# A two-layer attention block and a mixture of experts on one core: the first three head tiles multiply the residual without its norm, and large buffers share one start modulo 512 bytes

## Chip, cores and metric

One core of a Trainium2 chip. The metric is the device time of one execution in microseconds; the number of a kernel is the median over its runs. All arithmetic that matters is FP32, with matrix products as three products of operands split in a rounded high part and a low rest.

## What is computed

The reference runs `first_block` (two layers) and `second_block` (one layer) on 512 tokens of width 1024. The change touches the two layers of the first block. Cut to what matters:

```python
def rms_norm(x, g):
    y = xf * lax.rsqrt(jnp.mean(xf * xf, axis=-1, keepdims=True) + EPS)
    return (y * g.astype(jnp.float32)).astype(x.dtype)

def token_mixers(u, w_in, ...):
    proj = u @ w_in
    qa, ka, va, qi, ki, wi, qb, kb, vb, gate_a, gate_b = jnp.split(proj, ...)
    qa = apply_rope(rms_norm(qa.reshape(...), g_qa), cos, sin)
    qi = apply_rope(qi.reshape(bsz, length, H_I, D_I), cos, sin)
    ki = apply_rope(ki, cos, sin)
    ...
for i in range(DEPTH):
    u = rms_norm(h, g_mix_norm[i])
    h = h + token_mixers(u, w_in[i], ...)
    h = h + conv_ffn(rms_norm(h, g_ffn_norm[i]), w_up[i], conv_w[i], conv_b[i], w_down[i])
    ple_gate = jax.nn.sigmoid(rms_norm(h, g_ple_norm[i]) @ w_ple_gate[i])
    h = h + ple_gate * (p[i].astype(h.dtype) @ w_ple_proj[i])
```

The norm of a token is one number, so a product of the residual with its gain but without the norm can be scaled afterwards: (h * g * n) @ w = ((h * g) @ w) * n, with n one factor for each token. The indexer's key (ki) and queries (qi) have no norm of their own; they are the first three head tiles.

## The kernel before

**Layout.** Activations stand transposed: 128 channels on the partitions, 512 tokens along the row, eight slices k for a width of 1024. hT is the residual, XH and XL are the high and low part of what is multiplied. Weights come as blocks of up to 1 MB (eight slices of 256 columns, BLK = 2048 words a partition). SyncE loads block n into raw[n % 3] (`load_to`, L2320) once the last tile of block n-3 is done; ScalarE copies it to wh, rounded (`cuts_to`, L1948); VectorE subtracts it from raw, which gives wl in place (`cuts_to`, L1368). A tile (`tile`, L895) is 128 output channels: for each k three matmuls of 128x128 by 128x512, wh by high, wh by low, wl by high, all into one PSUM bank; it is 24 matmuls at a depth of eight slices. wh or wl is the stationary operand, the activation the moving one.

**Order of the work.** Each engine has one hand-written program, in which functions of the same name meet through semaphores (`Signal`, `Banks`). Nothing is planned by costs: what an engine does next is what its program says next. TensorE's program (L1283 on) is for each layer: `norm_sums` (column sums of squares, 8 products of one column, L950), `norm_row` (spreads the 512 norm factors over the partitions, L963), `first_projections` (L1009), `attention` with the gate tiles between its steps (L1118), `branches` (L1190), `linear` (output), `ffn` (L1220), `embed` and `ple` (L1248, L1276). `keep_warm` (L890) puts filler matmuls where TensorE would be idle.

**The norm ahead of a layer.** ScalarE squares the slices (`square_of`, L1955), VectorE adds them (`add_to_norm`, L1378); after `norm_sums` VectorE scales, ScalarE takes the root, VectorE the reciprocal (`root`, L1392 and L1963). Then `rms` (VectorE L1399, ScalarE L1985) works through the eight slices: VectorE writes U = h * gain * norm (L1407), ScalarE rounds U into XH (L1969), VectorE subtracts for XL (L1415). The first projection tile takes slice k when XL of k is there (`fresh`, L901), the later ones without a wait.

**first_projections.** s counts 16 head tiles: ki, qi0, qi1, ka, then queries and keys of both attentions. Tiles 0 to 2 are copied to the arena by ScalarE as they are (L2043); from tile 3 on it squares and scales them (L2045, L2046). After tile 2 TensorE multiplies two columns for the lambdas (L1062), which VectorE made at the head of its own `first_projections` (L1468 to L1470). SyncE swaps the halves of each head by DMA (`swap_halves`, L2329), GpSimd multiplies by sin and cos (L2309, L2310), VectorE adds (`rope`, L1560). The index scores need tiles 0 to 2 from s = 5 on; VectorE then picks the top 256 keys by repeated maximum and replacement (`choose`, L1539).

**Where things lie.** Per partition in this order: hT, XH, XL (16384 bytes each), raw, wh (24576 each), cst (2692 words), sml (849 words), arena (NAR = 15120 words), slots (94 words), owner (16), scr (17 x 512 words), tiny. Each starts at a multiple of 32 bytes. The arena is reused by stage: heads, values and masks at the word offsets of L661 to L663; the two parts of the attention outputs (OBH, OBL and, over QB and KB, oah, oal); in the feed-forward and gated stages QH, QL (words 0 and 4096), the moving operands of the up-projections and of `ple`; the embedding's high part at 12288. The down-projections and all input projections take XH and XL. In the expert stage at the end nearly all of these buffers are places for expert weights (PARTS, L798).

```python
        KI, QI, OBH, OBL = 0, 512, 0, 2048
        KA, WV, QA, MB = 4096, 4608, 4880, 6928
        QB, KB, VB = 8976, 11024, 13072
```

Of the kernel before, what the change touches and what calls it, by code (L numbers as in the profile page):

```python
# [17 lines left out]
D = 1024  # L18
KT = 8
# [148 lines left out]
def program(nc, A, out, sizes, cparts, stop=None):  # L168
# [3 lines left out]
    with ExitStack() as ctx:  # L172
# [11 lines left out]

        at = here()
# [18 lines left out]
        NAR = 15120  # L204
# [4 lines left out]
        owner = sb("owner", [1, 16], I32)  # L209
        at = here()  # L210
# [354 lines left out]
        u_done = Signal(sem("u_done"), [(r, k) for r in (0, 3, 6) for k in range(8) if r >= 6 or k < 7])  # L565
        xkeys = []
        for li in layers:
            xkeys += [(r, k) for r in (3 * li, ("mix", li), 3 * li + 1, 3 * li + 2) for k in range(8)]
# [83 lines left out]
        def u_ready(r, k):  # L652
            return u_done((r, k)) if r >= 6 or k < 7 else bank.empty(("spread", r))
# [8 lines left out]
        KA, WV, QA, MB = 4096, 4608, 4880, 6928  # L662
        QB, KB, VB = 8976, 11024, 13072  # L663
# [26 lines left out]
        RROW, UP = S_(5), [S_(3), S_(4), S_(6)]  # L690
        pp, ph, pl = A3(8192, 8), R3(12288, 2), R3(13312, 2)
# [188 lines left out]
        def tensor_engine(pe):  # L880
# [14 lines left out]
            def tile(key, w, c, xs, fresh=None, warm=0, among={}):  # L895

                ps = opened(key)
                keep_warm(ps, warm)
                h, l = w
                for i, (k, hi, lo) in enumerate(xs):  # L900
# [4 lines left out]
                    mm = pe.matmul(ps[0:c.stop - c.start, :], l[:, k, c], hi, start=False, stop=i == len(xs) - 1)  # L905
                    if i in among:
                        among[i]()
# [42 lines left out]
            def norm_sums(r):  # L950
# [3 lines left out]
                keep_warm(ps, 3 if r and r % 3 == 0 else 0)  # L954
# [53 lines left out]

            def first_projections(li):  # L1009
                n0 = PER_LAYER * li  # L1010
                def two_scores(pair):
# [11 lines left out]
                for s in range(21):  # L1023
# [5 lines left out]
                    if s < 16:  # L1029
                        n = n0 + (s // 2 if s < 4 else s // 2 + 1)  # L1030
                        if s % 2 == 0:
                            split(n)
                        c = slice(128 * (s % 2), 128 * (s % 2) + 128)
                        tile(("win", li, s), weights(n, 256), c, xs, (lambda k: x((3 * li, k))) if s == 0 else None,
                             2 if s == 0 and li else 0, {1: lambda: head_rows(li, s - 1), 5: lambda: head_columns(li, s - 1)}
# [7 lines left out]
                    elif s < 20:  # L1043
# [239 lines left out]
            pe.wait_ge(c_first, 16)  # L1283
            for li in layers:
                n0 = PER_LAYER * li
                norm_sums(3 * li)
                norm_row(3 * li)
# [77 lines left out]
        def vector_engine(dve):  # L1365
# [33 lines left out]
            def rms(r, gain):  # L1399
                root(("sum", r), 4, 1.0 / D, EPS, normcols(r), nroot, r, nrec)  # L1400
                key = ("spread", r)
                dve.wait_ge(*bank.full(key))
# [382 lines left out]
            def ple(m, n0, r):  # L1785
# [3 lines left out]
                def gated(k):  # L1789
# [7 lines left out]
                    if k >= 2:  # L1797
                        add_to_norm(r, k - 1)
# [1946 lines left out]
```

## Time and profile before

| | |
|---|---|
| median of 3 runs | 2735.25 us (2733.56 to 2735.48) |
| profiled execution, its own time | 2737.47 us |
| its span | 2736.1 us |
| TensorE, VectorE, ScalarE, GpSimd busy | 2581.3, 1508.6, 1094.3, 153.8 us |
| mean granted TensorE clock | 0.98 |
| first layer | 0 to about 864 us |
| second layer | about 864 to 1707 us |
| second block up to the experts | 1707 to 2395 us |
| experts | 2395 to 2640 us |
| end | 2640 to 2736 us |

PE is TensorE's matmuls, PEld its weight loads (they overlap), DVE VectorE, ACT ScalarE, POOL GpSimd, SPq SyncE's queue. Matmuls are pipelined: the listed duration of one is longer than the step from its start to the next start. A clock of 1.00 is 2.4 GHz; it can be granted at 2.4 or at 1.2 GHz.

### The profile page before, as it was taken

To read this page: it belongs to the slowest core of one execution; us is meant where nothing else is said; L and a number is where in the kernel's file an instruction comes from. 1 tells how busy PE (TensorE), PEld (TensorE's weight loads), DVE (VectorE), ACT (ScalarE), POOL (GpSimd) and SP (SyncE) were. 2 spreads that over 40 slices of the span, in tenths; PEclk is the share of its full clock that TensorE was granted. 3 is DMA by queue.
4 is the path that set the end of the run, shared out by engine and by line. 5 is a ranking of instruction groups with operands and counts; after the bars stand their busy time and mean duration, and the time that the engine had idled before them with its cause. 6 is when DMAs were issued, how large, how long until landed. Compare 5 with 4: busy or idle time off the path is not lost.

```text
span 2736.1 us, 35790 instructions
## 1 busy us (share of the span) xinstructions
PE 2581.3 (94%) x14600; PEld 1906.8 (70%) x14600; DVE 1508.6 (55%) x2596; ACT 1094.3 (40%) x1725; POOL 153.8 (6%) x133
## 2 busy tenths in 40 slices
PE   5999999999999989999999999999999989999777
PEld 4777678888887777778888887766766658733226
DVE  4787556646566698555747475445434525412227
ACT  3436544333344425653424243354332324233235
POOL 1310000000000320000000000000000000022210
PEclk9999999999999999999999999999999989999998
DMA  4322232232221322232222222312111124699991
GB/s 153 116 81 85 89 123 100 93 100 101 89 97 62 122 99 81 97 116 100 93 100 101 93 93 93 123 45 88 47 51 43 36 97 147 250 373 394 399 373 73
DMA packets 70283, 342.97 MB, mean 125 GB/s; under 512 B 11618, under 2 KB 12514, under 8 KB 37220
## 3 DMA queue, kind: packets, MB, share of 16 engines
q1 hardware_dynamic: 64996, 332.22, 34.2%
q0 software_dynamic: 5120, 8.40, 0.9%
q8 instruction: 119, 1.95, 0.3%
q14 instruction: 48, 0.39, 0.0%
HBM read 312.26 MB, written 28.31 MB: 124 GB/s over the span
## 4 chain that ended last, share of the span: by engine, by line
PE 78%; DVE 8%; SPq 4%; ACT 4%; DMA 3%; issue 2%; POOLq 0%; DVEq 0%; ACTq 0%
PE bank L903 14%; PE bank L905 14%; PE bank L904 14%; SPq L3461 4%; PE bank L1093 4%; PE bank L1095 3%; PE bank L1094 3%; PE bank L2431 2%; PE bank L3328 2%; PE bank L1137 2%; DVE wl L1374 2%; PE bank L1167 1%; PE bank L1157 1%; DMA raw<-in_WE 1%; ACT wh L1952 1%
## 5 line engine op out<-in xcount | busy, mean ns | idle before, releaser
L1374 DVE TENSOR_TENSOR wl<-raw,wh 128x2048 fp32r<-128x2048 f32 (+1 forms) x165 | 368.3, 2234 | 168.8 <-ACT wh L1952 167.7
L903 PE MATMUL bank<-arena_rounded,wh 128*128 128x512 f32 x1056 | 418.8, 397 | 3.4 <-DVE arena_rounded L1624 3.2
L905 PE MATMUL bank<-arena_rounded,wl 128*128 128x512 f32 x1056 | 417.5, 395 | 0.0
L904 PE MATMUL bank<-arena_rounded,wh 128*128 128x512 f32 x1056 | 417.4, 395 | 0.0
L1952 ACT ACTIVATE wh<-raw 128x2048 fp32r<-128x2048 f32 (+1 forms) x165 | 303.3, 1840 | 174.2 <-DMA raw<-in_W 174.1
L903 PE MATMUL bank<-XH,wh 128*128 128x512 f32 (+1 forms) x760 | 303.0, 399 | 4.8 <-DVE XL L1415 4.7
L904 PE MATMUL bank<-XL,wh 128*128 128x512 f32 (+1 forms) x760 | 297.5, 391 | 0.0
L905 PE MATMUL bank<-XH,wl 128*128 128x512 f32 (+1 forms) x760 | 297.2, 391 | 0.0
L903 PEld LDWEIGHTS bank<-arena_rounded,wh 128*128 128x128 f32 x1056 | 199.1, 189 | 52.8 <-issue 5.2
L905 PEld LDWEIGHTS bank<-arena_rounded,wl 128*128 128x128 f32 x1056 | 199.0, 188 | 47.4
L904 PEld LDWEIGHTS bank<-arena_rounded,wh 128*128 128x128 f32 x1056 | 199.2, 189 | 46.8
L1093 PE MATMUL bank<-XH,wh 128*128 128x512 f32 (+1 forms) x408 | 186.6, 457 | 0.0
L903 PEld LDWEIGHTS bank<-XH,wh 128*128 128x128 f32 (+1 forms) x760 | 142.8, 188 | 50.3 <-issue 12.6
L905 PEld LDWEIGHTS bank<-XH,wl 128*128 128x128 f32 (+1 forms) x760 | 142.8, 188 | 31.5
L904 PEld LDWEIGHTS bank<-XL,wh 128*128 128x128 f32 (+1 forms) x760 | 143.0, 188 | 29.3 <-issue 0.2
L1095 PE MATMUL bank<-XH,wl 128*128 128x512 f32 (+1 forms) x408 | 163.1, 400 | 0.0
L1094 PE MATMUL bank<-XL,wh 128*128 128x512 f32 (+1 forms) x408 | 163.1, 400 | 0.0
L1747 DVE TENSOR_TENSOR scr<-bank,scr 128x512 f32<-128x512 f32 x88 | 60.8, 691 | 140.2 <-PE bank L905 140.1
L2071 ACT ACTIVATE scr<-scr,tiny 128x128 f32<-128x128 f32 (+3 forms) x160 | 89.3, 559 | 102.3 <-DVE tiny L1599 102.1
L2167 ACT ACTIVATE scr<-scr,sml 128x512 f32<-128x512 f32 x88 | 71.8, 816 | 140.2 <-DVE scr L1747 140.2
L1093 PEld LDWEIGHTS bank<-XH,wh 128*128 128x128 f32 (+1 forms) x408 | 78.1, 191 | 50.6 <-issue 34.3
L3413 DVE TENSOR_TENSOR scr<-bank,scr 64x512 f32<-64x512 f32 x32 | 21.9, 683 | 163.8 <-ACT scr L3390 163.8
(540 smaller groups left out, 4191.2 us busy)
## 6 DMA issues: line engine op xcount, KB each, us to landing
raw<-in_W SPq DMA_DIRECT2D x153, 1024.0 KB, 4.8
arena<-in_WE SPq DMA_DIRECT2D x31, 1024.0 KB
wh_full<-in_WE SPq DMA_DIRECT2D x15, 1024.0 KB
raw<-in_WE SPq DMA_DIRECT2D x15, 1024.0 KB
gsave<-scr SPq DMA_DIRECT2D x48, 256.0 KB
scr<-gsave SPq DMA_DIRECT2D x48, 256.0 KB, 4.0
XH_full<-in_WE SPq DMA_DIRECT2D x10, 1024.0 KB
XL_full<-in_WE SPq DMA_DIRECT2D x10, 1024.0 KB
```

What stands on the lines that cost most here:

```text
L903: pe.matmul(ps[0:c.stop - c.start, :], h[:, k, c], hi, start=i == 0, stop=False)
L904: pe.matmul(ps[0:c.stop - c.start, :], h[:, k, c], lo, start=False, stop=False)
L905: mm = pe.matmul(ps[0:c.stop - c.start, :], l[:, k, c], hi, start=False, stop=i == len(xs) - 1)
L1093: pe.matmul(o, h[:, k, c], hi, start=k == 0, stop=False)
L1094: pe.matmul(o, h[:, k, c], lo, start=False, stop=False)
L1095: mm = pe.matmul(o, l[:, k, c], hi, start=False, stop=k == KT - 1)
L1374: w_lo.inc(dve.tensor_tensor(wl[:, i % 3, 0:k], raw[:, i % 3, 0:k], wh[:, i % 3, 0:k].bitcast(F32), ALU.subtract), i)
L1747: bank.emptied(dve.tensor_tensor(u, bank.ap(key), RROW, ALU.mult), key)
L1952: w_hi.inc(act.activation(wh[:, i % 3, 0:k], raw[:, i % 3, 0:k], ACT.Copy), i)
L2071: sexp.inc(act.activation(dst[:, 0:n], dst[:, 0:n], ACT.Exp, scale=-1.0, bias=c, accum_out=c_sum), (m, s, e))
L2167: aff.inc(act.activation((FV if which else FG)[q % 2][i], UP[(4 * q + 2 * which + i) % 3], ACT.Identity, scale=K(f"cw2{li}", f), bias=K(f" ...
L3461: moe.e_in[n % RING].inc(sync.dma_start(moe.place(i, part_), expert(i, part_)), n)
```

## The change

**Starts of the buffers.** 128 bytes are put ahead of hT and ahead of the arena, 64 ahead of scr, the arena becomes 112 words longer, and its parts QA, MB, QB, KB, VB move up by 112 words.

**Tiles 0 to 2 of each layer.** A new `raw_high` (ScalarE) and `raw_low` (VectorE) split h * gain, without the norm, into XH and XL: for the first layer at the very start as x lands, for the second between the steps of the gated projection before it. TensorE's new `raw_projections` multiplies tiles 0 and 1 together, slice by slice, then tile 2. `norm_sums` and `norm_row` move in between: in the second layer the sums after slice 3 and the spread after slice 5 of the two tiles, in the first layer the sums after both tiles and the spread after slice 3 of tile 2. VectorE copies the spread row to WROW (scr slice 15), makes U from it as before, and scales tiles 0 to 2 by it as it takes them out of PSUM (`raw_head`), two between slices, the third at the end. ScalarE overwrites slice k of XH when tile 2 has used it (`raw_used`). Tile 3 is now the first that takes the normed XH and XL. The lambda products stay at the head of VectorE's `first_projections`, which comes after all of `rms`, and TensorE's lambda matmul at s = 2 is now ahead of its first tile in that loop. The filler ahead of the norm sums and of tile 0 in the second layer goes. The root's table is loaded ahead of the first norm. SyncE loads the first weight block after the first quarter of x and the second block ahead of the constants, and block n0+3 ahead of the first swaps.

```diff
+        sb("front", [128, 32])
         at = here()
         hT = sb("hT", [128, KT, T])
...
-        NAR = 15120
+        NAR = 15232
+        sb("gap", [128, 32])
...
         owner = sb("owner", [1, 16], I32)
+        sb("behind", [128, 16])
...
-        KA, WV, QA, MB = 4096, 4608, 4880, 6928
-        QB, KB, VB = 8976, 11024, 13072
+        KA, WV, QA, MB = 4096, 4608, 4992, 7040
+        QB, KB, VB = 9088, 11136, 13184
...
+            def raw_projections(li):
+                n0 = PER_LAYER * li
+                r = 3 * li
+                keys = [("win", li, i) for i in range(2)]
+                split(n0)
+                ps = [opened(key) for key in keys]
+                h, l = weights(n0, 256)
+                for k, hi, lo in xs:
+                    pe.wait_ge(*x((("raw", r), k)))
+                    for i, key in enumerate(keys):
+                        c = slice(128 * i, 128 * i + 128)
+                        pe.matmul(ps[i], h[:, k, c], hi, start=k == 0, stop=False)
+                        pe.matmul(ps[i], h[:, k, c], lo, start=False, stop=False)
+                        mm = pe.matmul(ps[i], l[:, k, c], hi, start=False, stop=k == KT - 1)
+                        if k == KT - 1:
+                            bank.filled(mm, key)
+                    if li and k == 3:
+                        norm_sums(r)
+                    if li and k == 5:
+                        norm_row(r)
+                if li == 0:
+                    pe.wait_ge(c_first, 16)
+                    norm_sums(r)
+                split(n0 + 1)
+                tile(("win", li, 2), weights(n0 + 1, 256), slice(0, 128), xs, None, {} if li else {3: lambda: norm_row(r)},
+                     lambda mm, k: raw_used.inc(mm, (r, k)))
...
-                    if s < 16:
+                    if 3 <= s < 16:
...
+            def raw_low(r, k):
+                dve.wait_ge(*xh((("raw", r), k)))
+                x.inc(dve.scalar_tensor_tensor(out=XL[:, k, :], in0=hT[:, k, :], scalar=K(f"gmix{r // 3}", k),
+                                               in1=XH[:, k, :].bitcast(F32), op0=ALU.mult, op1=ALU.subtract), (("raw", r), k))
+            def raw_head(li, s):
+                key = ("win", li, s)
                 dve.wait_ge(*bank.full(key))
+                bank.emptied(dve.tensor_tensor(head_at(s), bank.ap(key), WROW, ALU.mult), key)
+            def rms(li):
+                r = 3 * li
+                norm_row(r, WROW)
                 for k in range(KT + 1):
...
+                    if k in (4, 5):
+                        raw_head(li, k - 4)
+                raw_head(li, 2)
...
+            for k in range(8):
+                if k == 2:
+                    cuts_to(0)
+                raw_low(0, k)
+            cuts_to(1)
             for k in range(1, 7):
                 add_to_norm(0, k)
...
+            def raw_high(r, k):
+                act.wait_ge(*h_ready(r, k))
+                xh.inc(act.activation(XH[:, k, :], hT[:, k, :], ACT.Copy, scale=K(f"gmix{r // 3}", k)), (("raw", r), k))
...
                 for k in range(KT):
+                    act.wait_ge(*(raw_used((r, k)) if k < KT - 1 else bank.full(("win", li, 2))))
                     high((r, k), k, U[k % 3], u_ready(r, k))
...
             for i in range(4):
                 quarter_in[i].inc(sync.dma_start(hT[:, 2 * i:2 * i + 2, :], A["xT"][:, 2 * i:2 * i + 2, :]), "x")
-            sync.dma_start(sml[:, :], A["small"]).then_inc(s_in, 16)
+                if i == 0:
+                    sync.dma_start(sml[:, :], A["small"]).then_inc(s_in, 16)
+                    load_to(0)
+            load_to(1)
             sync.dma_start(cst[:, 0:384], A["consts"][:, 0:384]).then_inc(c_first, 16)
-            load_to(0)
             sync.dma_start(cst[:, 384:n_const], A["consts"][:, 384:n_const]).then_inc(c_in, 16)
...
+                    if s == 0:
+                        load_to(n0 + 3)
```

## Rows read from the trace of the kernel before

**Rows 1.** The profile's page: busy us, share of the span, instructions, by engine
```profile
PE 2581.3 (94%) x14600; PEld 1906.8 (70%) x14600; DVE 1508.6 (55%) x2596; ACT 1094.3 (40%) x1725; POOL 153.8 (6%) x133
```
**Rows 2.** The page: chain that ended last, share of the span by engine
```profile
PE 78%; DVE 8%; SPq 4%; ACT 4%; DMA 3%; issue 2%; POOLq 0%; DVEq 0%; ACTq 0%
```
**Rows 3.** Stretches: from:to, us, then busy (count) by engine, PEclk, DMA share, GB/s
```profile
438.00:806.00 368.00, 368.00 (x1605) 299.73 (x1604) 225.39 (x253) 139.41 (x147) 0.00 (x0) 1.00 0.28 95
...
864.00:888.00 24.00, 21.65 (x81) 15.40 (x82) 11.77 (x24) 8.71 (x15) 2.56 (x2) 0.86 0.08 18
...
2395.00:2640.00 245.00, 209.33 (x1079) 77.44 (x1077) 54.65 (x92) 80.15 (x159) 57.66 (x62) 0.99 1.01 391
```
**Rows 4.** The page: groups; out<-moving,stationary, shapes, count | busy us, mean ns | idle before
```profile
L903 PE MATMUL bank<-arena_rounded,wh 128*128 128x512 f32 x1056 | 418.8, 397 | 3.4 <-DVE arena_rounded L1624 3.2
...
L903 PE MATMUL bank<-XH,wh 128*128 128x512 f32 (+1 forms) x760 | 303.0, 399 | 4.8 <-DVE XL L1415 4.7
...
L1093 PE MATMUL bank<-XH,wh 128*128 128x512 f32 (+1 forms) x408 | 186.6, 457 | 0.0
```
**Rows 5.** Timeline of TensorE, branches and feed-forward: start us, duration us, instruction
```profile
344.72 0.47 PE L903 MATMUL bank<-arena_rounded,wh 128*128 128x512 f32 x1 [1.61 <-DVE arena_rounded L1624]
...
389.11 0.39 PE L905 MATMUL bank<-arena_rounded,wl 128*128 128x512 f32 x1
...
567.95 0.40 PE L903 MATMUL bank<-arena_rounded,wh 128*128 128x512 f32 x1
...
657.32 0.39 PE L905 MATMUL bank<-arena_rounded,wl 128*128 128x512 f32 x1
657.55 0.39 PE L1214 MATMUL bank<-XH,wh 128*128 128x512 f32 x1
...
700.85 0.39 PE L905 MATMUL bank<-XH,wl 128*128 128x512 f32 x1
```
**Rows 6.** Timeline of the first layer's norm and first projection
```profile
13.36 1.91 ACT L1952 ACTIVATE wh<-raw 128x2048 fp32r<-128x2048 f32 x1 [11.31 <-DMA raw<-in_W]
...
17.50 4.66 DVE L1383 TENSOR_TENSOR scr<-scr 128x512 f32<-128x512 f32 x6
...
29.31 1.40 DVE L1407 SCALAR_TENSOR_TENSOR scr<-hT,sml,bank 128x512 f32<-128x512 f32 x2 [1.21 <-PE bank L938]
...
31.59 0.76 PE L903 MATMUL bank<-XH,wh 128*128 128x512 f32 x1 [2.32 <-DVE XL L1415]
...
33.00 0.63 PE L903 MATMUL bank<-XH,wh 128*128 128x512 f32 x1
...
33.43 0.63 PE L904 MATMUL bank<-XL,wh 128*128 128x512 f32 x1
...
35.11 0.40 PE L905 MATMUL bank<-XH,wl 128*128 128x512 f32 x1
```
**Rows 7.** Timeline of the first layer: last lambda product, first matmul of tile 3
```profile
39.84 0.15 DVE L1470 TENSOR_TENSOR tiny<-sml 128x1 f32<-128x1 f32 x1
...
51.66 0.48 PE L903 MATMUL bank<-XH,wh 128*128 128x512 f32 x1
```
**Rows 8.** Timeline of the second layer's norm, and its tile 3
```profile
858.42 2.29 DVE L1374 TENSOR_TENSOR wl<-raw,wh 128x2048 fp32r<-128x2048 f32 x1
...
860.62 0.68 DVE L1805 TENSOR_TENSOR scr<-bank,scr 128x512 f32<-128x512 f32 x1
861.34 0.63 ACT L2198 ACTIVATE scr<-scr 128x512 f32<-128x512 f32 x1 [2.96 <-DVE scr L1805]
...
864.08 3.21 PE L959 MATMUL bank<-cst,scr 128*128 128x1 f32 x16 [2.07 <-DVE scr L1383]
...
891.57 0.48 PE L903 MATMUL bank<-XH,wh 128*128 128x512 f32 x1
```
**Rows 9.** Stretches of the first layer before and in the top-k choice, columns as in rows 3
```profile
31.00:88.00 57.00, 55.52 (x243) 42.08 (x244) 28.67 (x36) 24.34 (x35) 16.07 (x12) 1.00 0.33 102
...
136.00:148.00 12.00, 9.98 (x51) 8.76 (x52) 11.65 (x21) 4.03 (x6) 4.85 (x4) 0.86 0.16 31
```

More of the change, by code:

```diff
@@ L564, in program @@
         nrec = Signal(sem("nrec"), ALLN)
-        u_done = Signal(sem("u_done"), [(r, k) for r in (0, 3, 6) for k in range(8) if r >= 6 or k < 7])
+        u_done = Signal(sem("u_done"), [(r, k) for r in (0, 3, 6) for k in range(8)])
+        raw_used = Signal(sem("raw_used"), [(r, k) for r in (0, 3) for k in range(7)])
         xkeys = []
         for li in layers:
-            xkeys += [(r, k) for r in (3 * li, ("mix", li), 3 * li + 1, 3 * li + 2) for k in range(8)]
+            xkeys += [(r, k) for r in (("raw", 3 * li), 3 * li, ("mix", li), 3 * li + 1, 3 * li + 2) for k in range(8)]
         xkeys += [(r, k) for r in (6, ("mix", 2)) for k in range(8)]
@@ L652, in u_ready @@
         def u_ready(r, k):
-            return u_done((r, k)) if r >= 6 or k < 7 else bank.empty(("spread", r))
+            return u_done((r, k))
         def roped(li, t):
@@ L893, in keep_warm, with tile @@
                     pe.matmul(ps, ident, C("cos"), start=True, stop=True)
-            def tile(key, w, c, xs, fresh=None, warm=0, among={}):
+            def tile(key, w, c, xs, fresh=None, among={}, used=None):
                 ps = opened(key)
-                keep_warm(ps, warm)
                 h, l = w
@@ L905, in tile @@
                     mm = pe.matmul(ps[0:c.stop - c.start, :], l[:, k, c], hi, start=False, stop=i == len(xs) - 1)
+                    if used and i < len(xs) - 1:
+                        used(mm, k)
                     if i in among:
@@ L953, in norm_sums @@
                 ps = opened(key)
-                keep_warm(ps, 3 if r and r % 3 == 0 else 0)
+                keep_warm(ps, 3 if r == 6 else 0)
                 last, ready = (SQ[1], square((r, 7))) if r < 6 else (hT[:, 7, :], h_ready(r, 7))
@@ L1033, in first_projections @@
                         c = slice(128 * (s % 2), 128 * (s % 2) + 128)
-                        tile(("win", li, s), weights(n, 256), c, xs, (lambda k: x((3 * li, k))) if s == 0 else None,
-                             2 if s == 0 and li else 0, {1: lambda: head_rows(li, s - 1), 5: lambda: head_columns(li, s - 1)}
+                        tile(("win", li, s), weights(n, 256), c, xs, (lambda k: x((3 * li, k))) if s == 3 else None, {1: lambda: head_rows(li, s - 1), 5: lambda: head_columns(li, s - 1)}
                              if s in (8, 12) else {})
@@ L1798, in gated @@
                         add_to_norm(r, k - 1)
+                    if r == 3 and k:
+                        raw_low(r, k - 1)
                 for k in range(8):
@@ L2200, in ple @@
                         square_of(r, k - 1)
+                        if r == 3:
+                            raw_high(r, k - 1)
                 root_table()
                 square_of(r, 7)
-            cuts_to(0)
+                if r == 3:
+                    raw_high(r, 7)
+            act.wait_ge(s_in, 16)
+            for k in range(8):
+                if k == 2:
+                    cuts_to(0)
+                raw_high(0, k)
+            cuts_to(1)
             for k in range(8):
                 square_of(0, k)
-            cuts_to(1)
-            act.wait_ge(s_in, 16)
             act.wait_ge(c_first, 16)
+            root_table()
             for li in layers:
                 n0 = PER_LAYER * li
-                rms(3 * li)
+                rms(li)
                 first_projections(li)
```

42 lines of the change are left out of this document (17 added, 25 removed).

## Prediction

> **What bounds the kernel now.** I read the busy shares first, then the chain, then stretches, and only then single instructions. TensorE is busy 94% of the span against VectorE's 55% [rows 1], and the chain that ended last runs through it for 78% [rows 2]. In the two feed-forward stretches it never stops: 368.00 us busy of 368.00, VectorE at 61% [rows 3]. There a shorter TensorE instruction shortens the run one for one. The expert stretch is another matter: 391 GB/s and a DMA share of 1.01 over 245 us [rows 3], so nothing gained on TensorE inside it counts.
>
> What the groups of instructions hide is the pace. A matmul's own duration overlaps the next, so I read start to start. The second stretch of up-projections is 16 tiles of 24 matmuls, 384 in all, fed from the arena: from 567.95 to 657.55 it takes 89.60 us, 233.3 ns each. The 192 down-projection matmuls right behind it have the same shape, the same weight buffers and a moving operand in XH or XL: from 657.55 to 700.85 are 191 steps, 226.7 ns each [rows 5]. The branch projections, 192 matmuls fed from the arena, step at (389.11 - 344.72) / 191 = 232.4 ns. So an arena-fed matmul costs 5.7 to 6.6 ns more. The group holds 3 x 1056 = 3168 of them [rows 4].
>
> **Where the buffers lie.** Sizes in the code give it. hT, XH, XL, raw and wh are whole multiples of 512 bytes, so they and cst begin at one offset, call it a. cst (10768 bytes) and sml (3396), each rounded up to 32, put the arena at a + 14208 = a - 128 modulo 512, and scr too. QA, MB, QB, KB and VB lie another 64 bytes on, at a - 64. The gap of 128 bytes, the longer arena (60928 = 119 x 512) and 64 bytes behind owner bring arena, its parts and scr to a. The shift in front moves a itself by 128, for all alike. So after the change every moving operand stands to the weights as XH stands to wh now.
>
> **The change, part by part.**
> 1. *Common offset.* Two of the three up stretches of each layer step at 233.3 (384 and 288 matmuls, 1344 in both layers): 6.6 ns less each, 8.9 us. For the remaining 1824 (first up stretch, branches, embedding, gated projection) I take the branches' 232.4: 5.7 ns, 10.4 us. Together 19.3 us; I take 18.9, since the warmed XH pace beside other work is a little over 226.7. Bounds: 0 if the offset has nothing to do with it, 3168 x 6.6 = 20.9 us if all fall by the larger step. Nearest row to the new state is XH in the same stage, so I stay near the upper end. Cover: the DMA share is 0.28 and VectorE is at 61% there [rows 3], so TensorE stays the bound. FP32 transposes from scr may also gain; nothing in the rows separates them, below 2 us, counted 0.
>
> What speaks against this part is a rule: the Trainium skill, SBUF — State Buffer, section "SBUF: two separate sides", says contention is structural (the port pair shared by VectorE and GpSimd, or the AXI ports), that TensorE never waits on anyone, and its table gives LDWEIGHTS a second read port. All starts here are multiples of 32 bytes before and after, so by that page this part is worth nothing. The steps of rows 5 differ for equal shapes, which it does not explain; I follow the rows, and give the other case a chance below.
>
> 2. *First layer's start.* Now: the first weight block lands at 13.36, behind all of x; two cuts, seven square/add steps, sums, a table load inside the norm chain, then the first projection at 31.59, paced by VectorE; head tile 3 starts at 51.66 [rows 6, 7]. 3.8 MB had to land by 13.36; at 391 GB/s [rows 3] that is 9.6 us behind some 3.7 of start. In the new order (first quarter of x, sml, block 0, rest of x, block 1) block 0 has 2.0 MB before its end: about 8.8 to 9.2; x's last quarter 13; block 1 about 15.4; ones and identity 16. ScalarE's cut 1.9 and VectorE's 2.29 follow: TensorE starts near 13.4. Its 48 matmuls run first at the lower level (0.43 us a step at 33.00, each 0.63 long; 0.40 long by 35.11 [rows 6]) and then at 0.227: about 12.9 us, to 26.3. VectorE meanwhile does eight low parts (0.7, the rate of 29.31), the cut of block 1, six adds at 0.78, ready at 24.3: hidden. Sums 1.6 (half of 3.21, which was at the lower level [rows 8]): 28.0. Four slices of tile 2, spread, four more: 34.0.
> Now the new wait. VectorE copies the norm row (32.2), then runs the old eight-slice chain, 29.31 to 39.84 = 10.5 us [rows 6, 7], with three head scalings of 0.69 in it (the eviction at 860.62 is of that kind [rows 8]): 44.8. The lambda products stand behind that chain on VectorE, and TensorE's lambda matmul, which used to come behind tiles 0 to 2, is now ahead of tile 3 and waits for them: TensorE idles from 34.0 to about 45.2, tile 3 starts at 45.5. That is 6.2 earlier. The idle stretch lets the clock fall (a mean of 0.86 over the stretch around the second layer's norm, where TensorE idled [rows 3], so part of it at 1.2 and not 2.4 GHz); as after 31.59, some 3.3 us of work then go at the lower level, 1.6 lost. **Gain 4.6.** Behind the wait are tile 3 and all else of TensorE. Bounds: 6.2 if the clock holds, 1 if chain and clock are each 2 to 3 us worse.
>
> 3. *Second layer's start.* The products without the norm need only XH/XL of the residual, made during the gated projection: 8 x 0.63 on ScalarE [rows 8] and 8 x 0.7 on VectorE [rows 6], hidden for k up to 4. The last ones are not: two low parts push VectorE's cut at 858.42 and the eviction at 860.62 back by about 1.5; one more 0.63 goes ahead of the square of slice 7. TensorE, which now starts multiplying at 859.3 in place of idle filler, does four slices of both tiles (5.4 us), then waits some 1.4 for the squares; sums end at 867.9, four slices and spread at 874.0, tile 2 at 879.5. ScalarE may overwrite XH slice 0 only when tile 2 has used it (874.9), so VectorE's chain ends at about 886.6; tile 3 starts at 887.2, now 891.57 [rows 8]. 4.4 less 1.7 for the clock: **gain 2.7.** Bounds: -1 to 5.
>
> 4. *The rest.* Six ScalarE evictions move to VectorE; the rope swaps of heads 0 to 2 start near 40, are done by 52, and scores need them only some 10 us later. SyncE issues the same DMAs; block n0+3 now goes before the first swaps, at no cost since it waits for the same tiles. The added table load stands where ScalarE waits anyway. VectorE is the bound later, 11.65 busy of 12 us in the top-k stretch [rows 9]; it is busy only 28.67 of 57 us from 31 to 88 [rows 9], so that stretch starts as much earlier as TensorE does and passes the gain on.
>
> **Sum:** 18.9 + 4.6 + 2.7 = 26.2 us. The profiled execution took 2737.47 (span 2736.1); the median of the three runs is 2735.25, 2.2 lower, and I carry the difference over: 2737.47 - 26.2 = 2711.3 for a profiled one, 2709 for the median.
>
> **Rivals.**
> - *Common offset idle.* The 6 ns belongs to something else of the arena (its distance, what runs beside it). Parts 2 and 3 remain: 2735.25 - 7.3 = 2728. For: the page above. Against: the step is as rigid over 90 us with VectorE now busy, now idle, and changes at the very instruction where the operand changes. Chance 0.1.
> - *The lambda wait eats the early start.* If VectorE's chain runs 2 to 3 us longer and the clock takes twice as long to rise as after 31.59, parts 2 and 3 give 0 together: 2735.25 - 18.9 = 2716. For: TensorE idles twice for 8 to 11 us where it ran before. Chance 0.17.
> - *The change misses its offset*: a pad rounds otherwise, the arena stays off. Same time as the first rival; my byte count speaks against it. Chance 0.02, the same number.
> - *Slower:* the new common start, 128 bytes further, is itself a bad one and XH-fed matmuls take the arena's pace. They are 3 x (760 + 408) = 3504 in the two large groups [rows 4]: at 5.9 ns 20.7 us more, the arena's 18.9 not gained, 7.3 kept: 2735.25 + 13.4 = 2749. It decides once XH-fed steps rise by 2.1 ns with the arena unchanged. Nothing in the trace supports a dependence on the absolute start, but none shows a second one. Chance 0.04.
>
> **Numbers.** My forecast has 0.67: 2709, its own range 2703 to 2715. A range of 2701 to 2725 takes in the second rival, gains of up to 34 us if the first layer's start is better than I work out and the transposes join, and most of what lies between the cases; it leaves out the first, third and slower rivals. A measurement tells about 0.2% (5.5 us) from no change: slower than 2729.8 is not faster. The first rival lies just under that line, so I split it: faster 0.91, same 0.05, slower 0.04.
>
> **What would show it.** Right: in the up-projections steps of 226 to 228 ns and each feed-forward stretch about 6.5 us shorter; first TensorE matmul near 13.4; tile 3 at about 45.5 behind a wait on VectorE's lambda products, and about 4 us earlier in layer two before the shift from upstream. Wrong: an arena-fed step still at 232 or 233 (part 1), a pace of XH over 229 (the slower case), tile 3 of either layer no earlier than now (parts 2, 3), or TensorE waits in the feed-forward stretch.

## Result, and the profile after

The changed kernel takes 2715.5 us (median of 14 runs, 2706.5 to 2730.1) against 2735.4 for the kernel before (14 runs, 2729.9 to 2749.4): ratio 0.9921, interval 0.9906 to 0.9937. By the ratio that is 21.6 us less, between 17.2 and 25.7 (the two medians differ by 19.9), where 26.2 was forecast. The 2715.5 lie within the range of 2701 to 2725, but half a microsecond outside the forecast's own 2703 to 2715. The profiled execution took 2721.8 (span 2720.5), 6 us above the median, so its trace shows less than the whole gain.

The page of the kernel after: busy time, chain, and the groups that answer to [rows 1, 2, 4]. L903 of the kernel before is now L907.

```profile
PE 2564.9 (94%) x14590; PEld 1909.7 (70%) x14590; DVE 1536.6 (56%) x2620; ACT 1101.7 (40%) x1736; POOL 154.3 (6%) x133
...
PE 77%; DVE 9%; ACT 5%; SPq 4%; DMA 3%; issue 2%; POOLq 0%; DVEq 0%; ACTq 0%
...
L907 PE MATMUL bank<-arena_rounded,wh 128*128 128x512 f32 x1056 | 413.1, 391 | 3.6 <-DVE arena_rounded L1665 3.2
...
L907 PE MATMUL bank<-XH,wh 128*128 128x512 f32 (+1 forms) x728 | 292.5, 402 | 0.2 <-DVE XL L1704 0.2
```

TensorE is still the bound and has 16.4 us less to do. The mean of a single arena-fed matmul fell by 6 ns (397 to 391). The pace shows it better. PE's timeline of the kernel after at the second stretch of up-projections: start, duration, line and operation.

```profile
567.25 0.39 PE L907 MATMUL bank<-arena_rounded,wh 128*128 128x512 f32 x1
...
654.07 0.39 PE L909 MATMUL bank<-arena_rounded,wl 128*128 128x512 f32 x1
654.29 0.39 PE L1248 MATMUL bank<-XH,wh 128*128 128x512 f32 x1
...
697.59 0.39 PE L909 MATMUL bank<-XH,wl 128*128 128x512 f32 x1
```

The 384 arena-fed matmuls take (654.07 - 567.25) / 383 = 226.7 ns a step, where [rows 5] gave 233.3. The 192 fed from XH stay at (697.59 - 654.29) / 191 = 226.7. The difference between the two operands is gone. The branches now step at (390.06 - 346.68) / 191 = 227.1.

The heads next: PE of the kernel after, from its first matmul through the first layer's lambda wait to the last of the 72 matmuls behind it (tile 3, the 68-column tile `wv`, tile 4); then the same places of the second layer. The expectations below call these 72 "tiles 3 to 5".

```profile
13.46 0.80 PE L1027 MATMUL bank<-XH,wh 128*128 128x512 f32 x1 [13.46 <-DVE wl L1405]
...
33.59 0.39 PE L909 MATMUL bank<-XH,wl 128*128 128x512 f32 x1
...
46.00 0.56 PE L1096 MATMUL bank<-tiny,cst 128*128 128x2 f32 x2 [12.02 <-DVE tiny L1511]
46.42 0.77 PE L907 MATMUL bank<-XH,wh 128*128 128x512 f32 x1
46.99 0.63 PE L908 MATMUL bank<-XL,wh 128*128 128x512 f32 x1
...
64.90 0.40 PE L909 MATMUL bank<-XH,wl 128*128 128x512 f32 x1
...
881.28 0.56 PE L1096 MATMUL bank<-tiny,cst 128*128 128x2 f32 x2 [8.45 <-DVE tiny L1511]
881.70 0.77 PE L907 MATMUL bank<-XH,wh 128*128 128x512 f32 x1
...
900.64 0.39 PE L909 MATMUL bank<-XH,wl 128*128 128x512 f32 x1
```

TensorE starts at 13.46 and is done with tile 2 at about 34, then stands for 12.02 us before two tiny matmuls of the lambdas, and for 8.45 us in the second layer. What it waits for is the last of three products of one column at the end of VectorE's queue. VectorE's timeline of the kernel after:

```profile
31.26 0.69 DVE L1470 COPY scr<-bank 128x512 f32<-128x512 f32 x1 [2.71 <-PE bank L944]
31.99 1.42 DVE L1449 SCALAR_TENSOR_TENSOR scr<-hT,sml,scr 128x512 f32<-128x512 f32 x2
...
37.90 0.68 DVE L1440 TENSOR_TENSOR arena<-bank,scr 128x512 f32<-128x512 f32 x1
...
43.13 1.52 DVE L1453 TENSOR_TENSOR XL<-scr,XH 128x512 fp32r<-128x512 f32 x1 [0.16 <-ACT XH L2017]
44.57 0.68 DVE L1440 TENSOR_TENSOR arena<-bank,scr 128x512 f32<-128x512 f32 x1
45.17 0.14 DVE L1509 TENSOR_SCALAR tiny<-sml 128x1 f32<-128x1 f32 x1
45.23 0.56 DVE L1510 TENSOR_TENSOR tiny<-sml 128x1 f32<-128x1 f32 x1
45.71 0.15 DVE L1511 TENSOR_TENSOR tiny<-sml 128x1 f32<-128x1 f32 x1
```

**Where the time went.** I cut each profiled execution at marks that all kernels have: the first matmul of head tile 10 (the head ends; the expectations below call it head tile 8, but `wv` and the score products lie between), VectorE's first attention product (the top-k choice ends), the first branch projection (attention ends), the last arena-fed matmul of the gated projection (the rest ends). Lengths in us; each row is one execution.

| kernel | head 1 | top-k 1 | att. 1 | rest 1 | head 2 | top-k 2 | att. 2 | rest 2 | second block and end | span |
|---|---|---|---|---|---|---|---|---|---|---|
| before | 105.0 | 72.0 | 167.8 | 514.3 | 85.9 | 74.7 | 167.7 | 514.8 | 1033.9 | 2736.1 |
| after | 101.9 | 76.4 | 168.4 | 506.1 | 84.9 | 73.8 | 167.6 | 506.0 | 1035.4 | 2720.5 |
| after, second | 103.0 | 71.0 | 167.7 | 506.5 | 85.4 | 73.7 | 166.1 | 506.1 | 1030.9 | 2710.4 |
| after, third | 102.0 | 73.6 | 167.7 | 506.0 | 85.0 | 73.5 | 164.5 | 506.1 | 1032.1 | 2710.5 |
| offset alone | 104.6 | 73.3 | 166.1 | 506.9 | 85.7 | 74.5 | 164.5 | 506.7 | 1035.2 | 2717.5 |
| heads alone | 103.0 | 69.9 | 164.6 | 514.4 | 85.3 | 74.1 | 166.0 | 514.3 | 1036.2 | 2727.8 |
| lambda products first | 96.5 | 72.0 | 167.6 | 506.1 | 81.0 | 71.4 | 167.6 | 506.8 | 1038.5 | 2707.5 |
| filler in the wait | 100.7 | 73.7 | 167.6 | 506.5 | 82.0 | 74.6 | 166.0 | 505.5 | 1035.4 | 2712.0 |
| arena 256 bytes off | 104.7 | 72.8 | 164.5 | 506.0 | 84.5 | 73.0 | 166.0 | 506.1 | 1032.3 | 2709.9 |
| arena 32 bytes off | 104.7 | 73.3 | 166.0 | 515.1 | 85.7 | 73.9 | 168.6 | 515.4 | 1040.4 | 2743.1 |
| before, short rope | 104.7 | 66.0 | 166.1 | 514.4 | 85.7 | 65.9 | 166.1 | 514.6 | 1033.3 | 2716.8 |
| after, short rope | 101.4 | 66.0 | 167.7 | 506.8 | 82.6 | 66.0 | 167.6 | 506.8 | 1028.3 | 2693.2 |

Three things stand out. The two "rest" columns fall in two groups, 514.3 to 515.4 or 505.5 to 506.9, and lose 8.2 and 8.8 us with the change. The heads lose 3.1 and 1.0, but the rows with the old heads differ among themselves, from 104.6 to 105.0 and from 84.5 to 85.9. By the means of before, offset alone, 256 and 32 bytes off (104.76 and 85.44) and of after, its two repeats and heads alone (102.46 and 85.15), the new heads are worth 2.3 us in the first layer and 0.3 in the second, where the rows overlap. And the first layer's top-k choice, which the change does not touch, is 4.4 us longer in this execution, so that the branches start later than before, at 346.68 for 344.72 [rows 5]; it is 71.0 and 73.6 in two other executions of the same kernel.

The attention, untouched as well, has its own steps: 164.5, about 166 or about 167.7 us. They follow TensorE's granted clock. In the third execution of the changed kernel it is 167.7 at a mean of 0.98 in the first layer and 164.5 at 1.00 in the second. In all these executions the clock fell to 1.2 GHz never, once or twice at the start of that stage or inside it, and each time goes with some 1.6 us.

### The profile page after: what moved, and what is told of

It is laid out like the page before. It is cut to its first block, busy times and chain, and to the rows that moved or that the text cites. A ratio compares the mean times of both kernels' runs of the same rounds, so it can differ in the third digit from the quotient of the medians.

```text
span 2720.5 us, 35826 instructions
## 1 busy us (share of the span) xinstructions
PE 2564.9 (94%) x14590; PEld 1909.7 (70%) x14590; DVE 1536.6 (56%) x2620; ACT 1101.7 (40%) x1736; POOL 154.3 (6%) x133
## 4 chain that ended last, share of the span: by engine, by line
PE 77%; DVE 9%; ACT 5%; SPq 4%; DMA 3%; issue 2%; POOLq 0%; DVEq 0%; ACTq 0%
PE bank L907 13%; PE bank L909 13%; PE bank L908 13%; PE bank L1127 4%; SPq L3527 4%; PE bank L1128 3%; PE bank L1129 3%; PE bank L3394 2%; PE bank L2497 2%; PE bank L1171 2%; DVE wl L1405 2%; ACT wh L2000 1%; PE bank L1201 1%; PE bank L1191 1%; DMA raw<-in_WE 1%
## 5 line engine op out<-in xcount | busy, mean ns | idle before, releaser
L907 PE MATMUL bank<-arena_rounded,wh 128*128 128x512 f32 x1056 | 413.1, 391 | 3.6 <-DVE arena_rounded L1665 3.2
L909 PE MATMUL bank<-arena_rounded,wl 128*128 128x512 f32 x1056 | 411.7, 390 | 0.0
L908 PE MATMUL bank<-arena_rounded,wh 128*128 128x512 f32 x1056 | 411.6, 390 | 0.0
L907 PE MATMUL bank<-XH,wh 128*128 128x512 f32 (+1 forms) x728 | 292.5, 402 | 0.2 <-DVE XL L1704 0.2
L908 PE MATMUL bank<-XL,wh 128*128 128x512 f32 (+1 forms) x728 | 287.7, 395 | 0.0
L909 PE MATMUL bank<-XH,wl 128*128 128x512 f32 (+1 forms) x728 | 287.6, 395 | 0.0
L907 PEld LDWEIGHTS bank<-arena_rounded,wh 128*128 128x128 f32 x1056 | 198.7, 188 | 47.4 <-issue 5.1
L1127 PE MATMUL bank<-XH,wh 128*128 128x512 f32 (+1 forms) x408 | 187.1, 459 | 0.0
L907 PEld LDWEIGHTS bank<-XH,wh 128*128 128x128 f32 (+1 forms) x728 | 138.9, 191 | 40.6 <-issue 9.3
L1128 PE MATMUL bank<-XL,wh 128*128 128x512 f32 (+1 forms) x408 | 163.5, 401 | 0.0
L1129 PE MATMUL bank<-XH,wl 128*128 128x512 f32 (+1 forms) x408 | 163.3, 400 | 0.0
```

Of the source, the lines that this page charges most:

```text
L907: pe.matmul(ps[0:c.stop - c.start, :], h[:, k, c], hi, start=i == 0, stop=False)
L908: pe.matmul(ps[0:c.stop - c.start, :], h[:, k, c], lo, start=False, stop=False)
L1127: pe.matmul(o, h[:, k, c], hi, start=k == 0, stop=False)
L1128: pe.matmul(o, h[:, k, c], lo, start=False, stop=False)
L1129: mm = pe.matmul(o, l[:, k, c], hi, start=False, stop=k == KT - 1)
```

## Experiments

**Each half alone, and what the lambda wait costs.** Four kernels on one chip, beside the kernel before (2736.4, 17 runs). The offset alone:

```diff
+        sb("front", [128, 32])
-        NAR = 15120
+        NAR = 15232
+        sb("gap", [128, 32])
+        sb("behind", [128, 16])
-        KA, WV, QA, MB = 4096, 4608, 4880, 6928
-        QB, KB, VB = 8976, 11024, 13072
+        KA, WV, QA, MB = 4096, 4608, 4992, 7040
+        QB, KB, VB = 9088, 11136, 13184
```

> The kernel before with the new starts of the buffers alone; nothing of the heads or the order is changed. Theory (the relative start sets the pace): arena-fed steps fall from 232.4 to 233.3 ns to about 226.8, the time falls by 18 to 19.5 us, to about 2716.5. Rival (most of the gain is the new head of the layers): the pace falls the same but the time only by 10 or less, since VectorE's stretches take it back. Rival (start is idle): 0.

Measured 2718.2 (6 runs), ratio 0.9935, interval 0.9921 to 0.9950: 18 us less. The heads alone are the changed kernel with this diff taken back.

> The changed kernel with the old starts of the buffers: only the tiles without the norm and the new order. My prediction had -7.3 us for this (4.6 in the first layer, 2.7 in the second). The trace of the changed kernel says less: tile 3 of the first layer starts 5.2 earlier, but the branches of that layer start 2.0 later, since the top-k stretch of VectorE lost it. By that theory this kernel is at -2 to -5 us, with arena-fed steps at 232 to 233 ns. If the two parts help each other, this and the offset alone sum to less than the whole change.

Measured 2734.0 (12 runs), ratio 0.9991, interval 0.9977 to 1.0006: 2.4 us less, not told from nothing. Its arena-fed steps stay at 232.5 and 233.3, its XH-fed ones at 226.7. The heads still lose 2.0 and 0.6 us in the table. So the offset carries most of the result. What the new order of the heads gives is less sure: 2.4 us by this run, a third of the 7.3 forecast and not told from nothing; 5.7 by the ratios of the whole change (0.9914, below) and of the offset alone (0.9935), whose intervals overlap. For the rest, the lambda products were moved from the head of VectorE's `first_projections` to the head of its norm:

```diff
                 r = 3 * li
+                dve.tensor_tensor(tz(16), K(f"lam{li}", 0), K(f"lam{li}", 1), ALU.mult)
+                lam_m.inc(dve.tensor_tensor(tz(17), K(f"lam{li}", 2), K(f"lam{li}", 3), ALU.mult), li)
                 norm_row(r, WROW)
```

> The changed kernel with the two lambda products put ahead of VectorE's norm chain, so that TensorE's lambda matmul no longer waits for that chain and tile 3 starts right behind tile 2, slice by slice. Theory (this wait costs the whole run time): tile 3 starts near 34.3 instead of 46.4 and ends near 46 instead of 53, the same in the second layer: 5 to 12 us faster than the changed kernel. Rival (VectorE's own work from there to the end of the top-k stretch is the bound): within 2 us of the changed kernel.

Measured 2704.5 (5 runs), ratio 0.9885, interval 0.9868 to 0.9902, beside 2711.2 (6 runs), ratio 0.9914, interval 0.9899 to 0.9929, for the changed kernel itself:

> The changed kernel once more, on the same chip as the three others, as their measure. 2706 to 2722, about 20 below the kernel before.

The two intervals just overlap; the medians are 6.7 us apart, and the trace says where from. PE of the kernel with the lambda products first:

```profile
33.32 0.39 PE L909 MATMUL bank<-XH,wl 128*128 128x512 f32 x1
33.55 0.28 PE L1096 MATMUL bank<-tiny,cst 128*128 128x2 f32 x2
33.97 0.50 PE L907 MATMUL bank<-XH,wh 128*128 128x512 f32 x1
...
35.24 0.50 PE L907 MATMUL bank<-XH,wh 128*128 128x512 f32 x1 [0.30 <-DVE XL L1455]
```

Tile 3 starts at 33.97 in place of 46.42 and then follows VectorE's slices, a group of three matmuls for each, with waits between, here of 0.30. The head is 5.4 us shorter than in the changed kernel's own profile, the second layer's 4.0. This is the fastest kernel of the study that computes all of it, 31.9 us below the one before on that chip.

**Which starts matter.** Three kernels, one run each, beside one run of the kernel before (2738.4). First only the 128 bytes ahead of hT, which move all large buffers alike:

```diff
+        sb("front", [128, 32])
         at = here()
         hT = sb("hT", [128, KT, T])
```

> The kernel before with the 128 bytes in front of all buffers alone: every start moves by 128 bytes, none moves against another. Theory (only the relative start counts): arena-fed steps stay at 232.4 and 233.3 ns, XH-fed ones at 226.7, the time stays. Rival (the common start of 256 modulo 512 is itself a good one): arena-fed steps fall. Slower rival of the prediction: XH-fed steps rise to 232 or more.

Measured 2735.0. Steps from arena 232.4 and 233.3, from XH 226.7 to 226.9, as before. A common start 128 bytes further on changes no step, which ends my slower rival. Then the offset alone with the arena a further 256 bytes on, and a further 32 bytes on:

```diff
-        sb("gap", [128, 32])
+        sb("gap", [128, 96])
```

> The offset-alone kernel with a gap of 384 bytes in place of 128, so that arena and scr lie 256 bytes modulo 512 from the weights. Theory of a row of 512 bytes: the step is that of any other misfit, 232 to 234 ns, and the gain of 18 us is gone. Rival (256 bytes are the period): 226.7 ns as at 0.

```diff
-        sb("gap", [128, 32])
+        sb("gap", [128, 40])
```

> The offset-alone kernel with a gap of 160 bytes, so that arena and scr lie 32 bytes from the weights modulo 512. If the cost comes with any misfit, steps are at 230 to 234 ns; if it grows with the distance, between 226.7 and 229.

Measured 2711.2 at 256 bytes and 2744.4 at 32. PE of the kernel with 256 bytes between, the same stretch as above:

```profile
562.54 0.39 PE L906 MATMUL bank<-arena_rounded,wh 128*128 128x512 f32 x1
...
649.35 0.39 PE L908 MATMUL bank<-arena_rounded,wl 128*128 128x512 f32 x1
```

and of the kernel with 32 bytes between, with the XH-fed stretch behind:

```profile
567.78 0.40 PE L906 MATMUL bank<-arena_rounded,wh 128*128 128x512 f32 x1
...
657.15 0.40 PE L908 MATMUL bank<-arena_rounded,wl 128*128 128x512 f32 x1
657.38 0.40 PE L1217 MATMUL bank<-XH,wh 128*128 128x512 f32 x1
...
700.72 0.39 PE L908 MATMUL bank<-XH,wl 128*128 128x512 f32 x1
```

The first has (649.35 - 562.54) / 383 = 226.7 ns, the second 233.3, and its XH-fed ones (700.72 - 657.38) / 191 = 226.9. So 256 bytes of difference are as good as none, where "modulo 512" had me expect a loss; and 32 bytes cost as much as the 128 of the kernel before. There is no slope with the distance: where the starts differ by 0 or 256 bytes the step is 226.7, where they differ by anything else tried it is 231.6 or more. The unmatched step is not one value, though. In the branches of the kernel before, whose parts are 64 and 128 bytes off, groups of twelve matmuls step at 231.6 and 232.3 by turns, with 32 bytes at 233.3; and within the stretch of 233.3 of the kernel before single steps alternate between 229 and 237 to 238, while matched ones are all 226 or 227. At 2.4 GHz 226.7 ns are 544 cycles, 512 columns and 32 more; 233.3 ns are in the mean 560, 512 and 48 more. Why is not shown. Only 0, 32, 128 (64 for the parts over QB and KB) and 256 bytes were tried.

**What lengthens the top-k choice.** The suspicion came from VectorE and GpSimd side by side. VectorE of the kernel after:

```profile
108.56 3.54 DVE L1577 SCALAR_TENSOR_TENSOR arena<-scr,arena 128x512 f32<-128x512 f32 x2
112.02 1.77 DVE L1606 TENSOR_TENSOR arena<-arena,scr 128x512 f32<-128x512 f32 x1
...
120.33 1.39 DVE L1596 TENSOR_SCALAR arena<-arena 128x256 f32<-128x256 f32 x1
121.75 1.39 DVE L1598 TENSOR_TENSOR arena<-arena,cst 128x256 f32<-128x256 f32 x1
123.06 1.64 DVE L1587 TENSOR_TENSOR arena<-arena,cst 128x384 f32<-128x384 f32 x1
124.74 0.56 DVE L1590 MAX8 tiny<-arena 128x8 f32<-128x384 f32 x1
```

GpSimd of the same execution:

```profile
109.79 1.76 POOL L2371 TENSOR_TENSOR scr<-scr,cst 128x512 f32<-128x512 f32 x1
...
121.52 1.33 POOL L2372 TENSOR_TENSOR arena<-arena,cst 128x512 f32<-128x512 f32 x1
122.82 1.47 POOL L2371 TENSOR_TENSOR scr<-scr,cst 128x512 f32<-128x512 f32 x1
124.25 1.60 POOL L2372 TENSOR_TENSOR arena<-arena,cst 128x512 f32<-128x512 f32 x1
```

VectorE of the kernel before at the same instructions:

```profile
121.60 0.28 DVE L1555 TENSOR_SCALAR arena<-arena 128x256 f32<-128x256 f32 x1
121.91 0.42 DVE L1557 TENSOR_TENSOR arena<-arena,cst 128x256 f32<-128x256 f32 x1
122.25 0.55 DVE L1546 TENSOR_TENSOR arena<-arena,cst 128x384 f32<-128x384 f32 x1
```

The same three instructions take 1.25 us before and 4.42 after, where rope products of GpSimd run beside them. Before, GpSimd had ended one at 117.49 and began the next at 122.89, just behind the three. To take the meetings away, both products were cut to one column, in the kernel before and in the changed one. That leaves out 511 of 512 columns of rope's two multiplications in every head, so these two runs compute something else than the reference.

```diff
-pool.tensor_tensor(RU[t % 6], RU[t % 6], C("sin"), ALU.mult)
+pool.tensor_tensor(RU[t % 6][:, 0:1], RU[t % 6][:, 0:1], C("sin")[:, 0:1], ALU.mult)
-pool.tensor_tensor(head_at(t), head_at(t), C("cos"), ALU.mult)
+pool.tensor_tensor(head_at(t)[:, 0:1], head_at(t)[:, 0:1], C("cos")[:, 0:1], ALU.mult)
```

> The kernel before with GpSimd's two products of the rotary embedding on one column in place of 512; left out are the other 511 columns of both products, so heads are not rotated. It keeps every wait and every other instruction. Theory (VectorE's instructions with two operands in SBUF wait for GpSimd's): the long ones among them in the top-k stretch, 1.4 to 1.9 us in place of 0.3 to 0.75, are short, and the first attention product comes 5 us or more earlier than in the kernel before. Rival (they are long for another reason): they stay long.

> The changed kernel with the same part left out. Theory: without GpSimd's products nothing eats the early start in the top-k stretch, so the first attention product of the first layer is as much earlier than in the short-rope kernel before as the head tiles 8 to 11 are, 3 to 5 us, and the branches of layer one too; all told 22 to 27 us faster than the short-rope kernel before. Rival (VectorE's own work there takes the gain whatever GpSimd does): first attention product within 1 us of the other's, and all told 19 us.

Measured 2718.2 (5 runs, 0.9938, interval 0.9901 to 0.9974) and 2694.1 (4 runs, 0.9833, interval 0.9797 to 0.9868), against 2738.5. VectorE of the changed kernel with short rope products:

```profile
116.00 0.29 DVE L1596 TENSOR_SCALAR arena<-arena 128x256 f32<-128x256 f32 x1
116.33 0.42 DVE L1598 TENSOR_TENSOR arena<-arena,cst 128x256 f32<-128x256 f32 x1
116.67 0.55 DVE L1587 TENSOR_TENSOR arena<-arena,cst 128x384 f32<-128x384 f32 x1
```

The choice takes 66.0, 65.9, 66.0 and 66.0 us in the two kernels and two layers, against 69.9 to 76.4 in all other rows of the table. So the meetings cost 4 to 10 us a layer. The traces bear it out instruction by instruction: the choice is some 130 VectorE instructions in every kernel, and in the other profiles those that overlap a product of GpSimd take 3.5 to 9.6 us longer in all than the same ones here (9.6 in the stretch of 76.4, 3.5 in that of 69.9), the remaining ones under 0.1. Without the meetings the two kernels' choice is equal, and the head's gain reaches the first attention product whole (170.6 and 167.4, 3.2 us). It does not reach the branches whole, as was expected: they start at 336.8 and 335.1, only 1.7 apart, because the attention between took 166.1 at a granted clock of 0.99 in the one execution and 167.7 at 0.98 in the other. The changed kernel is 24.1 us faster than the one before here too. The change itself does not make the choice longer, and the profile of 76.4 was an unlucky meeting: the means of the table's rows are 72.8 with the old heads and 72.8 with the new in the first layer, 74.0 and 73.5 in the second.

**The same meetings stand in the way of the lambda products.** GpSimd's first rope products come earlier with the new heads, at 42.66 for 45.55, and fall on the end of VectorE's chain ahead of TensorE's wait. GpSimd of the kernel after:

```profile
42.66 1.44 POOL L2371 TENSOR_TENSOR scr<-scr,cst 128x512 f32<-128x512 f32 x1 [42.20 <-DMA scr<-arena]
44.06 1.71 POOL L2372 TENSOR_TENSOR arena<-arena,cst 128x512 f32<-128x512 f32 x1
```

Beside them stand the last low part, 1.52 at 43.13, and a lambda product, 0.56 at 45.23 (both shown above). VectorE of the changed kernel with short rope products, the same two:

```profile
44.22 0.69 DVE L1453 TENSOR_TENSOR XL<-scr,XH 128x512 fp32r<-128x512 f32 x1 [0.16 <-ACT XH L2017]
...
45.49 0.15 DVE L1510 TENSOR_TENSOR tiny<-sml 128x1 f32<-128x1 f32 x1
```

TensorE's wait there is 10.79 us in the first layer and 7.21 in the second, 1.2 less than 12.02 and 8.45. The second layer's head is 3.1 us shorter than in the short-rope kernel before (82.6 and 85.7), where with full rope products the gain is 1.0 at most.

The Trainium skill, SBUF — State Buffer, section "SBUF: two separate sides", says that VectorE and GpSimd share a pair of ports as an exclusive lock, taken by VectorE in a two-port mode or with two SBUF inputs against a GpSimd instruction that reads SBUF. This case agrees: 0.28, 0.42 and 0.55 us become 1.39, 1.39 and 1.64 beside GpSimd's products. The first of them has one input, and no run here shows in which mode it ran; MAX8 keeps its 0.56 though a GpSimd product runs beside it (124.25).

**What the fallen clock costs.** Filler matmuls in TensorE's wait for the lambdas, 17 in the first layer and 12 in the second, beside the changed kernel once more:

```diff
                         ps = opened(("lam", li))
+                        for _ in range(12 if li else 17):
+                            pe.matmul(ps[:, 0:384], ident, cst[:, 0:384], start=True, stop=True)
                         pe.wait_ge(*lam_m(li))
```

> The changed kernel with filler matmuls (17 in the first layer, 12 in the second, 384 columns each) ahead of TensorE's wait for the lambda products, so that it is busy for most of the 12.0 and 8.5 us in which it now idles. Theory (a fallen clock takes 2 to 3 us of each head start): tiles 3 to 5 of both layers, 72 matmuls, step at 228 to 230 ns in place of 260 and 267, and head tiles 8 to 11 come 2 us earlier in each layer; 2 to 5 us faster than the changed kernel. Rival (VectorE's norm chain, not the clock, sets where those tiles end): steps fall, but the later marks and the time do not move.

> The changed kernel once more, beside the filler on the same chip: 2710 to 2716, steps of tiles 3 to 5 at 260 and 267 ns. If GpSimd's meeting with VectorE is what varies from one execution to the next, its stretch from head tile 8 to the first attention product is again another one between 69 and 77 us, in place of 72 to 73.5 in all executions with the old head.

Measured 2712.0 (4 runs, 0.9902, interval 0.9880 to 0.9924) and 2711.6 (4 runs, 0.9905, interval 0.9886 to 0.9924). The clock over the wait, from the stretches: first the kernel after, then the one with filler (columns as in [rows 3]).

```profile
31.00:46.00 15.00, 2.98 (x15) 2.17 (x13) 14.45 (x24) 6.87 (x10) 3.34 (x3) 0.71 0.14 35
```

```profile
31.00:47.00 16.00, 15.11 (x55) 9.53 (x53) 14.29 (x24) 6.88 (x10) 3.17 (x3) 1.00 0.17 48
```

PE of the kernel with filler, the first and the last of the 72 matmuls of the first layer:

```profile
47.33 0.48 PE L907 MATMUL bank<-XH,wh 128*128 128x512 f32 x1
...
63.65 0.40 PE L909 MATMUL bank<-XH,wl 128*128 128x512 f32 x1
```

The 72 matmuls take 16.32 us with filler and (64.90 - 46.42) = 18.48 without: 2.2 us lost to a clock at 1.2 GHz for the first eleven or so. In the second layer it is 16.3 against 18.94, 2.6. The heads become 1.3 and 3.0 us shorter than in the third execution of the changed kernel, but the total does not show it: the stages that the filler doesn't touch are together 5.8 us longer in its profile (2712.0 - 2710.5 + 4.3), which is within what they differ by between other executions. So the loss is real at its place, but the 2 to 5 us that the theory gave the whole run are not seen; what the repair is worth to it stays open, since the intervals of the two comparisons are 10 and 12 us wide.

## Why the prediction was right, point by point

- **Common offset: 18.9 forecast, about 18 measured.** Steps fell from 233.3 to 226.7 and from 232.4 to 227.1, as its stretch-by-stretch working had them. Summed over the five stretches of a layer (from the first to the last matmul of each) it is 8.7 us, twice, and 1.0 in the second block: 18.3. The offset alone measured 18. The small excess of the forecast is in the embedding and gated stretch, where I took 5.7 ns and the steps fell by 4.7 (234.5 to 229.8). The reading behind it, that the step differs by operand and not by what runs beside it, was right, and its rival "common offset idle" is out. The Trainium skill, SBUF — State Buffer, section "SBUF: two separate sides", says that TensorE never waits on anyone. The prediction had taken from it that this part might be worth nothing, and that does not follow: with no other engine involved, the step depends on where the moving operand starts beside the weights.
- **The period.** My byte count went by 512, as the change does. It holds, but 256 would have done; nothing in the trace of before could tell the two.
- **First layer's start: 4.6 forecast, 3.1 in the profile of after, 2.0 to 3.0 in three others.** The first matmul came at 13.46 (13.4 forecast), the norm row left PSUM at 31.95 (32.2), tile 2 ended at 34.0 (34.0). The term that came out too small is VectorE's chain: tile 3 at 46.42 and not 45.5. From the copy to the last lambda product it takes 31.95 to 45.86 = 13.9 us and not 12.6. The last low part takes 1.52 (0.69 otherwise), and the three lambda operations take 0.7 for 0.3: 1.2 us of meetings with GpSimd, which the sum did not have, and which are gone with short rope products. And the clock took 2.2 us, not 1.6. 51.66 - 46.42 = 5.2, less 2.2, is 3.1 within rounding, the table's figure.
- **Second layer's start: 2.7 forecast, 1.0 measured, 0.3 by the means.** `ple` ends at 852.75 for 859.04, so 6.3 of tile 3's 9.9 us (891.57 to 881.70) come from upstream. It is 3.6 us earlier of itself, not 4.4, and the clock takes 2.6, not 1.7. Here the term was mis-sized in both its parts. With short rope products the head is 3.1 us shorter: the wait is 1.2 us less without the meetings, and the clock takes 1.5 there and not 2.6.
- **"That stretch starts as much earlier as TensorE does and passes the gain on".** It starts earlier, but passes on only what the meetings with GpSimd leave: their spread of 5 us between executions is larger than both heads' gain. I had read VectorE as busy 11.65 of 12 us [rows 9] and not asked how much of that was waiting. With the meetings gone the gain does pass on, as far as the first attention product.
- **The rival of the lambda wait** (2716, heads worth nothing) is, by the time alone, as near as one can get: 2715.5 was measured, and the heads alone are not told from nothing. That the result also lies near the forecast is in part the width of the range. The traces set the degree: the wait eats the larger part of what the order could give, not all of it. With two tiny products moved, the heads are 5.4 and 4.0 us shorter and the medians 6.7 apart.
- **The slower rival** (an absolute start that is bad) is out by the run that moved all starts alike.

By their ratios the three comparisons put the changed kernel 21.6, 23.5 and 26.0 us below the kernel before (0.9921, 0.9914, 0.9905). The forecast's 26.2 lies above all three, within the intervals of the last two and just outside that of the first. It fits what was too high: 3 to 5 us in the heads, and about 1 or less in the offset.

## What to carry to other kernels

Where two equal matmuls differ in pace by operand, compare where the operands start: with moving and stationary starts a multiple of 256 bytes apart, each 512-column step was some 6 ns shorter here, 18 us over 3168 of them; only differences of 0 and 256 bytes were seen to be good. When a tile is moved ahead of a wait, look through what else now stands behind that wait: three products of one column at the end of a queue of VectorE held TensorE for 12 us, and to issue two of them first shortened the heads by more (5.4 and 4.0 us) than the new order itself had (3.1 and 1.0). A stretch in which VectorE is busy throughout may be waiting on GpSimd within its instructions; compare the durations of equal instructions before calling it bound.

## What was not expected of the hardware

- The pace of a 128x128 by 128x512 matmul depends on the relative start of its two operands: 226.7 ns at 0 and at 256 bytes, 231.6 to 233.3 at 32, 64 and 128. A misfit of 32 bytes costs as much as any other tried.
- VectorE's meetings with GpSimd in the top-k stretch vary from one execution of the same kernel to the next by up to 5 us, and cost 4 to 10 us a layer in all. A VectorE instruction with a single SBUF operand (0.28 us alone) took 1.39, and a product of one column (0.15 alone) 0.56.
- Two idle stretches of TensorE, of 12.02 and 8.45 us, cost 2.2 and 2.6 us of clock behind them; the shorter one cost more. In three other executions of the same heads, read in the same way, the loss was 2.2 to 2.6 us behind the longer and 1.4 to 2.7 us behind the shorter, so its size is not set by the wait's length alone. What sets it stays open.
- The attention stage of one and the same kernel takes 167.7 us at a granted clock of 0.98 and 164.5 at 1.00: part of the spread between executions is the clock's.
